# Reordering the stick-breaking chain, two stage starts and the difference on VectorE in a one-core decoder layer

## The reference, cut to what matters

```
blk = rows[:, idx] + pe[:, None, :]
return jax.nn.gelu(blk @ w1) @ w2
```

```
z = q . k / 8
log_1m = where(mask, log_sigmoid(-z), 0)
suffix = reverse_cumsum(log_1m) - log_1m
a = where(mask, exp(log_sigmoid(z) + suffix), 0);   o = a @ v
```

## Time and profile before

| what | us |
|---|---|
| median of 3 runs (lowest, highest) | 2608.1 (2602.7, 2609.49) |
| the profiled execution's own time | 2617.39 |
| its span, first to last instruction | 2615.8 |
| prompt attention, from the first steady slot | 672 of it |
| TensorE busy, whole span | 2303.3 (88%) |
| VectorE, ScalarE, POOL busy | 1229.1, 811.3, 619.7 |

### The profile page before, as it was taken

The page is one execution under the profiler, slowest core; times in us unless marked ns, Lnnn a source line. Parts: engine busy times, 40 slices in busy tenths (PEclk is TensorE's granted clock), DMA queues, the critical chain, the costliest instruction groups (busy, mean ns, idle before and its releaser), DMA issues. The chain is left out here.

```text
span 2615.8 us, 42372 instructions
## 1 busy us (share of the span) xinstructions
PE 2303.3 (88%) x12990; PEld 1758.7 (67%) x12990; DVE 1229.1 (47%) x1968; ACT 811.3 (31%) x1464; POOL 619.7 (24%) x643
## 2 busy tenths in 40 slices
PE   8899993799997728888899999697999999999998
PEld 2444441655553426667677777576999999999998
DVE  1778784333333215667655666664111111135553
ACT  2122211333330004555545555422111111123332
POOL 0998984222201511221222121000000000000000
PEclk9999996799998868989978898898999999999999
DMA  7688877988861486544554363222211111122110
GB/s 249 201 260 267 265 250 224 141 119 110 109 117 31 89 207 170 145 121 121 157 130 122 102 167 104 90 81 68 74 46 47 48 44 48 44 73 73 62 45 25
DMA packets 266555, 316.94 MB, mean 121 GB/s; under 512 B 59450, under 2 KB 174564, under 8 KB 266044
## 3 DMA queue, kind: packets, MB, share of 16 engines
q1 hardware_dynamic: 205724, 244.10, 33.8%
q0 software_dynamic: 16288, 43.31, 9.5%
q10 hardware_dynamic: 44368, 27.40, 3.6%
HBM read 283.00 MB, written 36.44 MB: 122 GB/s over the span
## 5 line engine op out<-in xcount | busy, mean ns | idle before, releaser
L234 POOL TENSOR_TENSOR key_products<-key_pages,sb_q_rows 128x512 f32<-128x512 f32 x256 | 341.5, 1376 | 83.4 <-DMA key_pages<-in_cache_sb_kv 59.9
L382 PE MATMUL pp<-w_in_sb,xT_sb 128*128 128x512 f32 (+3 forms) x864 | 355.1, 571 | 6.4 <-DMA w_in_sb<-in_w_in 6.4
L2010 PE MATMUL pg<-h_turned_hi,w_gu_hi 128*128 128x344 f32 x1056 | 338.3, 320 | 9.8 <-DVE h_turned_lo L2058 9.8
L2012 PE MATMUL pg<-h_turned_hi,w_gu_lo 128*128 128x344 f32 x1056 | 338.2, 320 | 0.0
L2011 PE MATMUL pg<-h_turned_lo,w_gu_hi 128*128 128x344 f32 x1056 | 338.0, 320 | 0.0
L382 PEld LDWEIGHTS pp<-w_in_sb,xT_sb 128*128 128x128 f32 (+1 forms) x864 | 156.5, 183 | 195.8 <-issue 188.5
L659 PE MATMUL ph_c<-rows_turned,w_cmp 128*128 128x510 f32 (+1 forms) x576 | 252.0, 564 | 15.5 <-ACT rows_turned L683 12.1
L2053 DVE TENSOR_TENSOR w_gu_lo<-late,w_gu_hi 128x512 fp32r<-128x512 f32 x88 | 60.9, 692 | 402.1 <-ACT w_gu_hi L2023 402.1
L942 POOL TENSOR_SCALAR late<-late 128x128 f32<-128x128 f32 (+3 forms) x64 | 105.3, 1646 | 559.1 <-DVE late L1204 559.1
L2121 POOL DMA_DIRECT2D out_y_prompt<-y_rows x32 | 17.5, 546 | 904.9 <-DVE y_rows L2179 904.9
L2139 PE MATMUL py<-w_down_hi,act_hi 128*128 128x256 f32 x704 | 202.6, 288 | 16.6 <-DVE w_down_lo L2196 16.6
(11 more groups left out here) (286 smaller groups left out, 4195.6 us busy)
## 6 DMA issues: line engine op xcount, KB each, us to landing
key_pages<-in_cache_sb_kv SPq DMA_DIRECT2D x256, 256.0 KB, 3.1
late<-in_cache_sb_kv SPq DMA_DIRECT2D x256, 256.0 KB, 3.0
late<-in_w_gate_up SPq DMA_DIRECT2D x88, 256.0 KB, 2.9
late<-in_cache_nsa_kv SPq DMA_DIRECT2D x128, 128.0 KB, 6.1
late<-in_cache_nsa_kv POOLq DMA_DIRECT2D x128, 128.0 KB, 5.5
late<-in_w_down SPq DMA_DIRECT2D x4, 2816.0 KB, 10.6
w_in_sb<-in_w_in SPq DMA_DIRECT2D x5, 2048.0 KB, 17.6
scratch_T_hi<-turned_hi ACTq DMA_DIRECT2D x8, 896.0 KB
```

The lines of the kernel that those rows point to most:

```text
L234: eng.tensor_tensor(prod[:, m % PR], kr[:, m % KR], qb[:, b % 2], ALU.mult).then_inc(multiplied, 1)
L382: mm = eng.matmul(pp[0:R, m % 4, 0:b - a], xT[:, u, k, 0:R], w[:, k, a:b], start=(k == 0), stop=(k == KT - 1))
L2010: eng.matmul(pg[:, e, c, 0:CW], w_hi[:, h, j, :], hT_hi[:, k, cols], start=k == 0, stop=False)
L2012: mm = eng.matmul(pg[:, e, c, 0:CW], w_lo[:, h, j, :], hT_hi[:, k, cols], start=False, stop=k == KT - 1)
```

## The change

Three places change.

1. Compression: the six weight loads move from SP's queue to ACT's, so that SP starts with the page table; TensorE turns the prompt's four pairs first, and the wait for the weights, the position rows' turn and the bias product come behind them; VectorE's and ScalarE's matching steps move behind their copies of the prompt's pairs.
2. Start of the prompt attention: SP issues the mask constants first; VectorE waits for them first and sets the constant tiles behind `consts_set`; POOL waits for the first head's six loads before it issues the ten loads of head 1.
3. The stick-breaking chain: ScalarE does absolute value and exponential both in the first slot and the logarithm in the second; VectorE scans in the third slot, after `out`; the subtraction (`difference`) comes at the head of the fourth slot, ahead of that slot's maximum and copies; `stick_exp` moves from the first slot of the next group to the end of the fourth slot of its own.

```
 compress, SyncE (these lines move to ScalarE's program, unchanged):
-                for kk, s in enumerate("kv"):
-                    eng.dma_start(pe[:, kk, :], io[f"pe_cmp_{s}"][0].rearrange("(m r) d -> m (r d)", r=2)).then_inc(w_loaded, 16)
-                    eng.dma_start(w1[:, kk], io[f"w_cmp1_{s}"][0].rearrange("(a j p) n -> p a j n", a=2, p=P)).then_inc(w_loaded, 16)
-                    eng.dma_start(w2[:, kk], io[f"w_cmp2_{s}"][0]).then_inc(w_loaded, 16)
 compress, TensorE:
                 def first():
                     for q in range(4):
                         turn_pair(None, q)
+                    eng.wait_ge(w_loaded, 16 * 6)
...
+                    eng.wait_ge(bias_saved, 1)
 attend_prompt, SyncE (these three lines come ahead of the queries' loads):
+                eng.dma_start(masksf[:, :, :], io["c_masks"]).then_inc(masks_loaded, 16)
+                eng.dma_start(cmaskf[:, :, :], io["c_cmask"]).then_inc(masks_loaded, 16)
+                eng.dma_start(rowok[:, :], io["c_rowok"]).then_inc(masks_loaded, 16)
 attend_prompt, GpSimd:
                 load_head(0, 0, slice(6, 10))
+                eng.wait_ge(first_loaded, 96)
                 load_head(1, 1)
 attend_prompt, ScalarE:
                     if s % 4 == 0:
                         if not (zero(N) and s < 4):
-                            stick_exp(N, s)
                             eng.wait_ge(scan_done, k)
                         eng.wait_ge(z_copied, k + 1)
                         eng.activation(lg[:, 0:w], zs[s // 4 % 2][:, 0:w], ACT.Abs)
+                        eng.drain()
+                        eng.activation(lg[:, 0:w], lg[:, 0:w], ACT.Exp, scale=-1.0)
                     elif s % 4 == 1:
                         eng.drain()
-                        eng.activation(lg[:, 0:w], lg[:, 0:w], ACT.Exp, scale=-1.0)
-                    elif s % 4 == 2:
-                        eng.drain()
                         eng.activation(lg[:, 0:w], lg[:, 0:w], ACT.Ln, bias=1.0).then_inc(log_done, 1)
+                    elif s % 4 == 3:
+                        stick_exp(N, s)
 attend_prompt, VectorE:
                     eng.tensor_tensor_scan(rev(dd), rev(lg), rev(rl), 0.0, ALU.add, ALU.add).then_inc(scan_done, 1)
+
+                def difference(N, s):
+                    w = width(FRONT[s - s % 4])
                     eng.drain()
                     eng.tensor_tensor(dd[:, 0:w], zs[s // 4 % 2][:, 0:w], dd[:, 0:w], ALU.subtract).then_inc(logw_ready, 1)
...
                     for s in range(U):
+                        if s % 4 == 3:
+                            difference(N, s)
                         stat(N, s)
                         if not (zero(N) and s < 2):
                             save_groups(eng, N, s - 2, 0)
                         if not (zero(N) and s < 3):
                             out(N, s - 3)
-                        if s % 4 == 3:
+                        if s % 4 == 2:
                             scan(N, s)
```

More of the change, by code:

```diff
@@ L597, in _ @@
             def _(eng):
[L598 to L607, removed]
                 def turn_pair(b, q):
@@ L671, in first @@
                         turn_pair(None, q)
+                    eng.wait_ge(w_loaded, 16 * 6)
+                    for kk in range(2):
+                        mm = eng.transpose(pv[:, kk * 16:kk * 16 + 16], pe[:, kk, :], ident[0:16, 0:16])
+                    mm.then_inc(pe_turned, 1)
+                    eng.wait_ge(pe_saved, 1)
+                    for kk in range(2):
+                        for m in range(16):
+                            mm = eng.matmul(ph[:, 0, kk:kk + 1], w1[:, kk, m // 8, m % 8, :], peT[:, kk, m:m + 1], start=(m == 0), stop=(m == 15))
+                    mm.then_inc(hidden_done, 1)
+                    eng.wait_ge(bias_saved, 1)
                 phases(eng, first, phase, values_product)
@@ L728, in first @@
                         save_pair(eng, None, 1, q)
+                    eng.wait_ge(pe_turned, 1)
+                    eng.tensor_copy(peT[:, :, :], pv[:, 0:32].rearrange("p (k m) -> p k m", k=2)).then_inc(pe_saved, 1)
+                    eng.wait_ge(hidden_done, 1)
+                    eng.tensor_copy(peb[:, :], ph[:, 0, 0:2]).then_inc(bias_saved, 1)
                 phases(eng, first, phase, save_values)
@@ L732, in _ @@
             def _(eng):
-                eng.wait_ge(bias_saved, 1)
+                for kk, s in enumerate("kv"):
+                    eng.dma_start(pe[:, kk, :], io[f"pe_cmp_{s}"][0].rearrange("(m r) d -> m (r d)", r=2)).then_inc(w_loaded, 16)
+                    eng.dma_start(w1[:, kk], io[f"w_cmp1_{s}"][0].rearrange("(a j p) n -> p a j n", a=2, p=P)).then_inc(w_loaded, 16)
+                    eng.dma_start(w2[:, kk], io[f"w_cmp2_{s}"][0]).then_inc(w_loaded, 16)
                 def phase(b, u, nb, nu, before):
@@ L1114, in stick_exp @@
                 def stick_exp(N, s):
-                    w, k = width(FRONT[(s - 4) % U]), N * NSTICK + s // 4 - 1
+                    w, k = width(FRONT[s - 3]), N * NSTICK + s // 4
                     eng.wait_ge(logw_ready, k + 1)
-                    if not (zero(N) and s < 8):
-                        m = back_of(s - 8)
+                    if not (zero(N) and s < 4):
+                        m = back_of(s - 7)
                         eng.wait_ge(turned, N * G + (m // U) * G + G0[m % U + 1])
@@ L1182, in _ @@
             def _(eng):
+                eng.wait_ge(masks_loaded, 48)
+                eng.tensor_copy(identb[:, :], ident[:, :])
+                eng.tensor_copy(masks[:, :, :], masksf[:, :, :])
+                eng.tensor_copy(cmask[:, :, :], cmaskf[:, :, :]).then_inc(consts_set, 1)
+                eng.memset(vx[:, :, :, :, HD:HD + 1], 1.0)
                 eng.memset(ones[:, :], 1.0)
```

32 lines of the change are left out of this document (9 added, 23 removed).

## The result

The changed kernel takes 2747.0 us, median of four runs (2733.2 to 2755.0); the kernel before took 2608.8 us beside it. The ratio is 1.0516, 95% interval 1.0455 to 1.0577: slower by 138 us where 62 were forecast, and outside the range that was given. The profiled execution took 2745.9 us (span 2744.3), 128.5 us more than that of before.

What follows compares the result with a forecast made beforehand. TensorE, busy for 88% of the span, was taken as the bound, other engines mattering only through its waits. Chain +43, clock +25 and starts -6 sum to +62 us on 2608.1, giving 2670 us, range 2612 to 2736.

Steps and rivals of the forecast that it cites:

- What goes: Prompt attention: TensorE's waits for stick weights (16.6 us) and VectorE's copies (9.9 us) go in full, together 26.5 us.
- The chain, +43: Prompt attention: scan and subtraction delay the win maximum, so TensorE waits; net of removed waits +43 us (23 to 74).
- The clock, +25: Prompt attention: longer stalls raise the lower-clock share from 22% to 33%, at a third: +25 us (0 to 55).
- clock goes much further: Rival, prompt attention: 45% at the lower clock, chain costs 30 us and clock 55, giving 2687 us; chance 25%.
- Compression, -4, bounds -7.5 to +3: Compression's start: earlier page loads win at most 7.5 us of waits, late weights lose up to 3; taken as -4.
- Prompt-attention start, -2: Start of prompt attention: masks earlier, but keys and values still waited for; 0 to 16.9 us gained, taken as -2.
- room on the win path: Rival, prompt attention: TensorE's work hides the delayed win maximum, leaving only gains, 2576 us; chance 10%.
- no change: Rival, whole kernel: starts and removed stalls give back all that the chain costs, 68 us; chance 4%.
- the clock stays as it is: Rival, prompt attention: the lower-clock share does not grow, only chain and starts count, 2645 us; chance 20%.
- The range: Whole kernel: 2612 us, chain and clock at lower bounds, to 2736 us, both at upper bounds.

Runs made afterwards that it cites:

- run 5: Changed kernel with unneeded TensorE transposes of the identity filling the waits ahead of the win transposes, t = 1 to 7: 2640.2 us, ratio 1.0082.
- run 2: Kernel before plus the compression's part alone (weight loads on ScalarE's queue, bias behind the prompt's pairs): ratio 1.0039.
- run 7: Kernel before plus the compression's part alone, with both queues starting the cached pages only after the six weight loads have landed: ratio 0.9998.
- run 3: Kernel before plus the changed start of the prompt attention alone (masks first, constants behind `consts_set`): ratio 0.9992.
- Run 11: Changed kernel with the subtraction halved by columns, one half at the fourth slot's head, the other behind its maximum, copies and output: 2714.0 us, ratio 1.0382.
- run 4: Changed kernel with the subtraction alone moved behind the fourth slot's maximum, copies and output: 2634.2 us, ratio 1.0072.
- run 10: Kernel before with filling transposes where TensorE waits, ahead of the win and stick transposes: 2590.6 us, ratio 0.9906.

## Why the prediction was right or wrong, step by step

- **What goes.** Right: the waits for the stick weights and for VectorE's copies are gone, and nothing else on the sb path took their place. One reason was misplaced: the stick exponential does not lie in front of the win transposes. At t = 7 it runs from 1178.36 to 1179.42, behind their start at 1178.12; the product of the win weights covers it.
- **The chain, +43.** Right in mechanism, close in size. From the sb product's end to the win transposes I had 5.25, 6.09, 6.04 and 5.86 us for t = 4 to 7; the trace has 4.97, 5.90, 6.05 and 5.68. Idle time grew by 34 us. That it is less than 43 fits the clock: 42% of the stretch, not 22, ran at the lower level, and my 55 us times the 58% at the upper one are 32. TensorE's own work covers more of the chain there: at t = 6, after a product that took 2.66 us and pages' products of 1.96, the wait is 0.23.
- **The clock, +25.** This is the step that failed; it measured 82. It has two factors. The share at the lower level, "from 22% to 33%", came from no row: it went to 42%. The price, "a us at the lower clock costs a third of a us", was taken from one window of 4 us with a granted clock of 0.60, which was not all at the lower level: over the 80% of the window that 0.60 means, a third is 0.42. From the whole stretch it is 82 us of busy time for 0.42 x 788 - 0.22 x 672 = 183 us more at the lower level, 0.45. At that price my own share would have given 34 us; the other 48 are the share. What could have been counted: before, 16 falls of 9 us, two a head, each worth 4 us. Had each of the four long waits of a head that I forecast brought a fall of its own, that would be 32 more and 130 us; my upper bound was 55. It became 13 more, and longer ones.
- **The rival "clock goes much further".** Its share, 45%, was close to the 42 that came; its 2687 us were too low by the same price, and it cut the chain to 30 us where 34 came. The Trainium skill, "TensorE: Matmul & The Clock Gate", section on psum-queue depth-cycling, has frequent micro-idles between groups of matmuls swing the clock. The trace agrees: 29 stretches at the lower clock where there were 16, and 9 in run 5, where the idles are filled.
- **Compression, -4, bounds -7.5 to +3.** Wrong in sign and outside its bound: +8.9 in the stage, some 10 in run 2. That the weights "share the DMA engines with the pages and may come later" was the mechanism, as run 7 shows. The bound of 3 us was the failed step: I had taken it as a part of TensorE's present wait for pages, which says nothing of how long 2.1 MB of weights (w1 alone is 1 MB each for keys and values, by its tile) take beside pages on full DMA engines. Ahead of the pages the weights had been there 11.4 us after the stage's first load (446.6 to 458.0 before); beside them it took 39.2 (449.1 to 488.4). The Trainium skill, "DMA: Bandwidth & Descriptors", section "Queues, rings and completion order", has each DMA engine take turns between its queues; worked out as an estimate, with two page queues beside the weights, that is three times 11.4, or 34 us. The trace is near that, with 39.2 us, and with the pages held back (run 7) the weights were there after 13.7. The first phase began 54.0 us after the stage's first load instead of 31.5; of these 22.5 us the rest of the stage made up 13.6. Most of that is the gain that the change was made for: before, TensorE's waits for cached pages are 11.7 us from 470 us to the stage's end (the earlier trace rows stops at 510 and so misses one of them), and the changed kernel has none, its pages having come while TensorE waited for the weights and made the bias. In run 7, where the pages come later, two such waits of 10.6 us in all are back.

```profile
PE px_c L621 <- DMA late<-in_cache_nsa_kv: 11.7, 3, 5.7
```

- **Prompt-attention start, -2.** No change (run 3), within the bounds. The masks were not what TensorE waited for in the end, as the keys and values come last out of a full queue either way.
- **The other rivals** had no support: for "room on the win path" and "no change" the win transposes came when the sum said, and "the clock stays as it is" fell with the clock's way from 0.89 to 0.79.
- **The range.** Its upper end takes 1 us off for the starts, whose own bounds allow 3 us of loss; with these it would have been 2740, still short of the measured time.

Open is what length of wait brings a fall. Run 11 suggests that the loss is not in proportion to the wait, but three points, each with its own spread, do not show it. The clocks of 0.76 for the chain alone and 0.79 for the whole change, with about the same waits, need not have a cause of their own: over the whole span the executions of the one are at 0.883 to 0.888 and those of the other at 0.882 to 0.894, and the two times are the same within their intervals.

## What to carry to other kernels

Count a new stall on TensorE twice: once for its length, and once for the fall of the clock behind it, here about 0.45 of the time then spent at the lower level and more than twice the stalls themselves. An instruction put ahead of a maximum, on an engine that is half idle, still costs if TensorE is what waits behind: of the subtraction's 48.5 us in the stretch 33 came back as waits, and with the clock some 115 us of time. With it behind that slot's maximum and copies (run 4) the whole change was 0.7% slower than the kernel before, of which the compression alone makes 0.4% (run 2). Loads on which a stage's first product hangs should not be started beside bulk loads that fill the DMA engines: here a queue of their own gave them no precedence (runs 2 and 7).

## What the runs showed of the hardware that I had not expected

- Work that nobody needs makes the kernel faster: 580 transposes took the changed kernel from a ratio of 1.0516 to 1.0082 (run 5), and in the kernel before 340 of them cut 0.9% (run 10), since the granted clock of the steady stretch rises from 0.79 to 0.93 and from 0.89 to 0.96.
- The same 4168 matmuls of that stretch were busy for 589 us at a clock of 0.92 and for 712 us at 0.76.
- The issue of one load of 32 KB, 128 rows of 256 bytes, held ScalarE's program for 12.5 us while the pages were moving; on SP, ahead of the pages, the issue on line 564 had taken 2.28 us, and from ScalarE's queue with the pages held back (run 7) it took 2.42.
